# Setup of a two-block layer kernel: modulation pieces in the order 0, 2, 1, 3, two projection units by halves of the inner index, and part of the late pieces summed on TensorE

## The reference, cut to what matters

```python
for l in range(DEPTH):
    ada = jax.nn.silu(c) @ w_ada[l] + b_ada[l]          # (1, 1024) @ (1024, 6144)
    sh1, sc1, g1, sh2, sc2, g2 = jnp.split(ada, 6, axis=-1)
    h = x * (1.0 + sc1) + sh1
    y = mixer_ab(h, w_in_ab, ...)                       # starts with h @ w_in, (256, 1024) @ (1024, 3072)
```

## Time and profile before

| | |
|---|---|
| median of 3 runs | 1678.25 us (1677.92 to 1686.55) |
| the profiled execution, its own time | 1678.13 us |
| its span | 1676.3 us, so 1.8 us lie around it |
| PE busy | 1612.7 us, 96% of the span |
| DVE busy | 1085.5 us, 65% |
| ACT busy | 804.9 us, 48% |
| first projection matmul starts | 44.35 us into the span |

### The profile page before, as it was taken

The page is one execution under the profiler, slowest core; times in us unless marked ns, Lnnn a source line. Parts: engine busy times, 40 slices in busy tenths (PEclk is TensorE's granted clock), DMA queues, the critical chain, the costliest instruction groups (busy, mean ns, idle before and its releaser), DMA issues.

```text
span 1676.3 us, 24647 instructions
## 1 busy us (share of the span) xinstructions
PE 1612.7 (96%) x9268; PEld 1347.2 (80%) x9268; DVE 1085.5 (65%) x1329; ACT 804.9 (48%) x1033; POOL 224.8 (13%) x300
## 2 busy tenths in 40 slices
PE   3999999998999999999999999999999999999999
PEld 2997788878887788778888978888888889878887
DVE  7788878877758546664556896454554546765554
ACT  1565534336555343454446655434454445664433
POOL 2101001000000000068936200000000002200000
PEclk9999999999999999999999999999999999999999
DMA  9976787884644755465554425555465554345552
GB/s 320 335 250 202 274 297 280 283 290 130 212 148 143 276 191 185 151 189 183 192 176 138 166 81 179 194 182 193 157 201 192 184 192 164 138 160 178 197 179 98
DMA packets 225750, 330.10 MB, mean 197 GB/s; under 512 B 10423, under 2 KB 187160, under 8 KB 225678
## 3 DMA queue, kind: packets, MB, share of 16 engines
q1 hardware_dynamic: 210480, 276.93, 49.6%
q0 software_dynamic: 14800, 52.06, 8.9%
q10 hardware_dynamic: 398, 0.11, 0.0%
HBM read 327.97 MB, written 1.09 MB: 196 GB/s over the span
## 4 chain that ended last, share of the span: by engine, by line
PE 74%; DVE 13%; DMA 7%; ACT 3%; issue 2%; SPq 0%; POOLq 0%; POOL 0%; DVEq 0%; ACTq 0%
PE bank L2786 35%; PE bank L2530 20%; PE bank L2518 7%; DMA s_late<-in_w_ada 5%; DVE s_late L1916 4%; DVE s_wL L1898 3%; PE bank L2488 3%; PE bank L2798 1%; DVE s_late L1928 1%; ACT s_wH L1458 1%; DMA s_mix<-in_w_ada 1%; PE bank L2500 1%; DMA s_raw<-in_w_ffn_in 1%; PE bank L2629 1%; PE bank L2585 1%
## 5 line engine op out<-in xcount | busy, mean ns | idle before, releaser
L1898 DVE TENSOR_TENSOR s_wL<-s_raw,s_wH 128x2048 fp32r<-128x2048 f32 x254 | 587.1, 2312 | 296.1 <-ACT s_wH L1458 295.6
L1458 ACT ACTIVATE s_wH<-s_raw 128x2048 fp32r<-128x2048 f32 x254 | 485.2, 1911 | 229.6 <-PE bank L2786 144.8
L2786 PE MATMUL bank<-s_wH,s_hH 128*128 128x512 f32 x1056 | 420.7, 398 | 11.2 <-DVE s_hL L2252 8.7
L2786 PE MATMUL bank<-s_wH,s_hL 128*128 128x512 f32 x1056 | 412.6, 391 | 0.0
L2786 PE MATMUL bank<-s_wL,s_hH 128*128 128x512 f32 x1056 | 412.0, 390 | 0.0
L2786 PEld LDWEIGHTS bank<-s_wH,s_hH 128*128 128x128 f32 x1056 | 198.7, 188 | 55.8 <-issue 8.3
L2786 PEld LDWEIGHTS bank<-s_wH,s_hL 128*128 128x128 f32 x1056 | 198.5, 188 | 42.6
L2786 PEld LDWEIGHTS bank<-s_wL,s_hH 128*128 128x128 f32 x1056 | 199.0, 188 | 39.9 <-issue 0.7
L2530 PE MATMUL bank<-s_wH,s_aH 128*128 128x512 f32 x496 | 194.2, 392 | 1.1 <-DVE s_hL L2020 0.9
L2530 PE MATMUL bank<-s_wH,s_aL 128*128 128x512 f32 x496 | 193.2, 390 | 0.0
L2530 PE MATMUL bank<-s_wL,s_aH 128*128 128x512 f32 x496 | 193.0, 389 | 0.0
(11 more groups left out here) (453 smaller groups left out, 2245.8 us busy)
## 6 DMA issues: line engine op xcount, KB each, us to landing
s_raw<-in_w_ffn_in SPq DMA_DIRECT2D x88, 512.0 KB, 4.8
s_raw<-in_ffn_w_gate SPq DMA_DIRECT2D x88, 512.0 KB, 3.7
s_raw<-in_ffn_w_up SPq DMA_DIRECT2D x88, 512.0 KB, 4.6
s_raw<-in_ffn_w_down SPq DMA_DIRECT2D x88, 512.0 KB, 4.2
s_late<-in_w_ada POOLq DMA_DIRECT2D x20, 2048.0 KB, 9.9
s_raw<-in_w_ffn_out SPq DMA_DIRECT2D x44, 512.0 KB, 5.1
s_raw<-in_w_in_ab SPq DMA_DIRECT2D x24, 512.0 KB, 9.2
s_raw<-in_w_in_cd SPq DMA_DIRECT2D x24, 512.0 KB, 4.6
```

What stands on the lines that cost most here:

```text
L1458: A(wH[:, slot, :], raw[:, slot, :], ACT.Copy).then_inc(hi_ready, 1)
L1898: TTn(wL[:, slot, :], raw[:, slot, :], wH[:, slot, :].bitcast(F32), ALU.subtract).then_inc(lo_ready, 1)
L2786: last = mm(bank[GU_BANK[tt]][:], h, w[:, k, :], start=(half == 0 and k == 0 and i == 0), stop=(half == 1 and k == 3 and i == 2), skip_gro ...
```

## The change

It does four things.

1. Pieces are taken in the order 0, 2, 1, 3 (`FIRST_COLS`). After two of them shift and scale of the lower 512 features are known, and `modulated(0)` makes `h` for these; `modulated(1)` does the upper ones at the end.
2. The first two projection units are loaded, split and multiplied by halves of the inner index (`half_unit`, `split_half`). The first halves of both stand ahead of the late pieces on all engines, the second halves behind them.
3. Of the two late pieces DVE makes six of eight multiply-adds (`ON_VECTOR`); PE makes the other two from the raw weights (`first_rows`: 8 matmuls of one column, in the same form as the sum at L2564), into the same accumulator.
4. The order of loads changes to match: `x` in two halves of columns, 1 MiB of projection weights ahead of the late pieces, one half piece through the third slot of `raw`. The third unit is loaded when DVE has read that half piece. POOL's load of the bias table also waits for the last piece. 8 matmuls on zeros (`keep_busy`) stand ahead of the second halves.

```diff
+        FIRST_COLS, ON_VECTOR = (0, 2, 1, 3), (8, 8, 6, 6)
@@ SP
             first_ada(0)
             first_ada(1)
-            sp.dma_start(x[:], a["x"][0].rearrange("(a p) d -> p a d", p=P)).then_inc(ev("x_in"), 16)
+            sp.dma_start(x[:, :, 0:512], x_in[:, :, 0:512]).then_inc(ev("x_in0"), 16)
+            half_unit(0, 0, ab_units[0])
+            half_unit(1, 0, ab_units[1])
             first_ada(2)
+            sp.dma_start(x[:, :, 512:D], x_in[:, :, 512:D]).then_inc(ev("x_in1"), 16)
             first_ada(3)
-            qkv("ab", a["w_in_ab"][0])
+            sp.wait_ge(ev("first_hi"), 2)
+            half_unit(0, 1, ab_units[0])
+            half_unit(1, 1, ab_units[1])
+            sp.wait_ge(ada_step[1], 12)
+            straight("ab", ab_units, 2)
@@ POOL, ahead of the bias table
+            pool.wait_ge(ev("ada_in31"), 16)
@@ ACT
             first_ada(0)
+            split_half(0, 0)
             first_ada(1)
+            modulated(0)
+            split_half(1, 0)
...
             first_ada(2)
-            split_py(0)
+            split_half(0, 1)
             first_ada(3)
-            transposed("ab", ...)
-            split_py(1)
+            modulated(1)
+            split_half(1, 1)
             split_py(2)
@@ DVE
+            def modulated(half):
+                r, g = TR["ab"], 2 * half
+                dve.wait_ge(ada_out[0], half + 2)
+                dve.wait_ge(ada_out[1], half + 2)
+                sc = adaC[:, 0, 8 + 4 * half:12 + 4 * half]
+                step(TS(sc, sc, 1.0, None, ALU.add))
+                dve.sem_inc(ev("scale_ready"), 1)
+                dve.wait_ge(tr_done, TRD["ab"] + g + 1)
+                for c in (2 * g, 2 * g + 1):
+                    last = TS(t32[:, c, :], bank[TURN_BANK["ab"][g]][:, (c % 2) * T:(c % 2) * T + T], adaC[:, 0, 8 + c:9 + c],
+                              adaC[:, 0, c:c + 1], ALU.mult, ALU.add)
+                last.then_inc(t32_ready, 1)
+                if half == 0:
+                    split_half(0, 0)
+                lower_part(r, g)
+                lower_part(r, g + 1)
+                split_half(1, half)
...
-            ada(0, 1, 2)
+            modulated(0)
...
+            ada(0, 1, 2)
...
             ada(1, 1, 3)
...
-            split_py(0)
-            transposed("ab", ..., whole=False)
-            split_py(1)
+            split_half(0, 1)
+            modulated(1)
             split_py(2)
@@ PE
+            def first_rows(b):
+                pe.wait_ge(ev(f"ada_in{b}1"), 16)
+                pe.wait_ge(ada_out[b % 2], b // 2 + 1)
+                for u in range(4):
+                    for k in range(ON_VECTOR[b], KC):
+                        mm(bank[(0, 3)[b % 2]][:, u:u + 1], first_raw[b][1][:, k - KC // 2, u * P:u * P + P], silc[:, k:k + 1],
+                           start=(u == 0 and k == ON_VECTOR[b]), stop=False, skip_group_check=True)
...
+                if l == 0:
+                    half_unit(0, 0)
+                    half_unit(1, 0)
+                    first_rows(2)
+                    turn_columns(1)
+                    ada(0, 0, 1, False, begun=True)
+                    first_rows(3)
+                    ada(0, 1, 1, False, begun=True)
+                    pe.wait_ge(ev("lam_part"), 3)
+                    mm(bank[1][:, 384:385], ones[0:1, :], lam[0:1, 5:6], start=True, stop=True).then_inc(ev("lam_part"), 1)
+                    pe.wait_ge(ada_out[0], 3)
+                    keep_busy(0, 8)
+                    half_unit(0, 1)
+                    half_unit(1, 1)
+                else:
+                    dense(0, 16)
```

More of the change, by code:

```diff
@@ L1194, in qkv, with straight @@
                                  col_unit(w, m * 1536 + j * 256 + 512 * u))
-            def straight(name, units):
-                for u, src in enumerate(units):
+            def straight(name, units, first=0):
+                for u, src in enumerate(units[first:], first):
                     n = START[name] + u
@@ L1513, in pair_direct, with transposed @@
                 return A(blocks(hH[:, c, :]), backwards(bank[b][:, 0:T]), ACT.Copy)
-            def transposed(name, scale=None, offset=0.0, groups=4, direct=False):
-                for g in range(groups):
+            def transposed(name, scale=None, offset=0.0, groups=4, direct=False, first=0):
+                for g in range(first, groups):
                     if not direct:
@@ L2563, in ada @@
                     for u in range(4):
-                        last = mm(b[:, u:u + 1], acc[:, u * P:u * P + P], ones_col, start=True, stop=True)
+                        last = mm(b[:, u:u + 1], acc[:, u * P:u * P + P], ones_col, start=not begun, stop=True, skip_group_check=begun)
                     last.then_inc(ada_mm[slot], 1)
@@ L2587, in turn_tile, with turn_columns @@
                         last.then_inc(tr_done, 1)
+            def turn_columns(half):
+                pe.wait_ge(ev(f"x_in{half}"), 16)
+                for tt in range(TT):
+                    for k in range(KC // 2 * half, KC // 2 * half + KC // 2):
+                        at = (k % 2) * T + tt * P
+                        last = pe.transpose(bank[TURN_BANK["ab"][k // 2]][:, at:at + P], x[:, tt, k * P:k * P + P], ident[:])
+                        if tt and k % 2:
+                            last.then_inc(tr_done, 1)
             def transposed(name):
                 busy = BUSY[name] if name in BUSY else (0, 0)
-                if name in ("ab", "cd"):
+                if name == "cd":
                     keep_busy(TURN_BANK[name][0], busy[0])
@@ L2724, in ada_turn, with half_unit @@
                     ada(l, slot, cnt, slot == 0, b)
-                dense(0, 16)
+                def half_unit(u, half):
+                    pe.wait_ge(*((lo_ready, u + (LO0 + 1)) if half else (ev("first_lo"), u + 1)))
+                    H, L = (w[:, u, :].rearrange("p (k c) -> p k c", k=KC) for w in (wH, wL))
+                    for pair in (2 * half, 2 * half + 1):
+                        if u == 0:
+                            pe.wait_ge(tl_ready, 4 * TR["ab"] + pair + 1)
+                        for ft in range(2):
+                            for k in (2 * pair, 2 * pair + 1):
+                                wh, wl = H[:, k, ft * P:ft * P + P], L[:, k, ft * P:ft * P + P]
+                                for i, (w, h) in enumerate(((wh, hH), (wh, hL), (wl, hH))):
+                                    last = mm(bank[4 + u][:, ft * T:ft * T + T], w, h[:, k, :], start=(ft == 0 and k == 0 and i == 0),
+                                              stop=(k == KC - 1 and i == 2), skip_group_check=True)
+                    if half:
+                        last.then_inc(unit_used, 1)
+                if l == 0:
[14 more added lines that the diff above has]
+                    dense(0, 16)
                 if l == 1:
@@ L2730, in mixer @@
                     narrow(0).then_inc(ev("fd_mm"), 1)
-                dense(16, LEAD)
+                dense(16 if l else 32, LEAD)
                 for s in range(STEPS):
@@ L2938, in _ @@
             ada(0, 0, 0, False)
+            turn_columns(0)
             ada(0, 1, 0, False)
```

60 lines of the change are left out of this document (32 added, 28 removed).

## The result

The changed kernel takes 1683.96 us (median of 7 runs, 1680.92 to 1690.41); the kernel before took 1679.64 beside it (7 runs). The ratio over all runs, which is not the quotient of the two medians, is 1.0032, interval 1.0019 to 1.0044: 0.3% slower, small but clear of zero, where 0.3% faster was forecast. The profiled execution took 1681.74, its span 1679.9 us.

A forecast was written before the change was run, and what follows sets the result against it. PE, busy 96% of the span, bounds the kernel, so earlier projections pay: 5.9 us won at units 0 and 1, of which 5.0 kept (DVE 3.5 plus slack 1.5). 1678.13 - 5.0 = 1673.1 us, range 1671.5 to 1675 (0.45).

The forecast's parts named there:

- First halves from 28.0, done 35.9: Setup: first projection matmul at 28.0 us; the 48 first-half matmuls take 7.9 us at the old pace, to 35.9.
- DVE done with piece 3 at 40.6: DVE in the setup: finishes the last late piece at 40.6 us, 2.1 later than before.
- Pace between 36 and 48, 0.10 each: PE's thin work between the halves: one-column sums at the fast level, 0.10 us each; the step trusted least.
- the first rival's middle case: Clock falls in PE's thin work towards 39 to 42: start 45.5 to 48.5, gain 1 to 3.5, 1676; chance 0.25, shared.
- Second halves from 45.3, units done 52.1, gain 5.9: Projections: second halves start at 45.3 us; units 0 and 1 done at 52.1 instead of 58.04, bounds 4.8 and 6.9.
- First late load 2.7 to 4.0 earlier, landing after 12.0, DVE 3.5 earlier: Load issued behind unit 0: leaves 2.7 to 4.0 us earlier, takes 12.0; DVE, waiting for it, moves by 3.5.
- the sum's own bounds: Behind unit 0: its 24 second-half matmuls end at 48.2 to 49.5 us, the late load 2.7 to 4.0 earlier.
- The byte bound: Loads up to unit 6: by bytes carried, unit 6 lands 5.2 us earlier at 366 GB/s or 0.5 at 320.
- PE keeps 5.0 at the second turn: Second turn: DVE's 3.5 us plus a slack of 1.5 let PE move 5.0 us before it waits.
- I know of nothing behind it that is tied to the clock and not to PE, DVE or these loads: Rest of the kernel behind the second turn: later DVE waits have room, so the 5.0 us gain lasts.

The follow-up runs named there:

- e5: Changed kernel with 10 multiplications of zeros ahead of the second turn, one piece of the modulation left out of the output: 1680.36 us, 1.0010.
- e7: The changed kernel again, unchanged, for a second profile and ten more runs: 1684.07 us, 1.0029 against the kernel before.
- e10: Changed kernel with 40 one-column multiplications more, computing nothing, in PE's wait near 377 us, which they overran: 1690.14 us, 1.0064.
- e12: e10 with 10 multiplications of zeros ahead of the second turn: 1688.39 us, 1.0053.
- e14: Changed kernel with 16 one-column multiplications that compute nothing in PE's wait near 377 us: 1679.57 us, 0.9999 against the kernel before.
- e15: e14 with 10 multiplications of zeros ahead of the second turn: 1678.65 us, 0.9999 against the kernel before.
- e16: Changed kernel with 10 multiplications of zeros ahead of PE's wait near 446 us (second mixer, fourth turn): 1683.82 us, 1.0025.
- e18: e15 with 5 more multiplications of zeros ahead of the fourth turn of the second mixer: 1678.06 us, 0.9999 against the kernel before.
- e13: Kernel before with 16 one-column multiplications that compute nothing in PE's wait near 377 us: 1685.18 us, 1.0036.
- e2: Changed kernel without the 8 multiplications of zeros ahead of the second halves: 1682.22 us, 1.0019 against the kernel before.
- e9: Kernel before with 40 one-column multiplications more, computing nothing, in PE's wait near 377 us, which they overran: 1685.24 us, 1.0040.

## Why the prediction was wrong

By its own steps:

- **First halves from 28.0, done 35.9:** 28.82 and 36.8. Right; 0.8 late from the start, since half of `x` landed at 21.6.
- **DVE done with piece 3 at 40.6:** 41.7. Right within 1.1.
- **Pace between 36 and 48, 0.10 each:** wrong from 40.6 on, the step trusted least and the first rival's middle case: a fall at 39 to 42, a start at 45.5 to 48.5 and a gain of 1 to 3.5 at unit 2. The last sums reached DVE 1.94 us late, and the zeros held PE from 48.2, when the first of DVE's two lower parts was done, to 49.2 (by the chain; the timeline has the first matmul behind them begin at 48.66, overlapping the last of them).
- **Second halves from 45.3, units done 52.1, gain 5.9:** 49.2, 55.5, gain 2.5. The start is 3.9 late (1.1 for DVE's work, 1.9 for the late sums, 0.9 for the zeros); 0.5 came back because only the first 9 matmuls were slow.
- **First late load 2.7 to 4.0 earlier, landing after 12.0, DVE 3.5 earlier:** wrong in sign in both profiles of the changed kernel. By the sum's own bounds the least should have been 1.9, since 21 slow matmuls of the 24 end at 50.3, not 49.5. It left 0.4 later (53.92; unit 0 was done as late as before) and took 13.2; in other executions of this setup it left at 49.9 to 54.1 and took 10.3 to 12.4. The second late load left 2.6 us behind it instead of 5.5 and landed inside the same full stretch. The byte bound (0.5 us of gain) was nearer than the sum's 3.5.
- **PE keeps 5.0 at the second turn:** it kept 2.3 up to it and lost them to a wait that reached 2.4 us. The price of that wait was not in the sum: a fall of the clock behind it. In the nine profiles that have this setup (the changed kernel, e5, e7, e10, e12, e14, e15, e16, e18) unit 2 began 2.4 to 5.2 us earlier than before, and at 84 us, behind the second turn, they stood between 2.2 us ahead and 4.1 behind.
- **"I know of nothing behind it that is tied to the clock and not to PE, DVE or these loads":** this step decided the sign. TensorE's program grew by 16 f32 multiplications (two passes and two weight loads each) and 8 of zeros. The fetches behind it came earlier relative to the work: one into the late load of 431.45; near 1004, where a fetch came 0.7 us earlier, a second stall appears.

So two steps failed, each by some 5 us. The gain of 5.0 did not last: with the fetches moved (e14, e15, e18) the changed setup is level with the kernel before (0.9999 each, at widest 0.9988 to 1.0010), where the forecast was 0.997. And the code, a term that the sum did not have, cost the rest: 1.0029 to 1.0032 against 0.9999.

The sum with what was measured: the changed kernel is 0.7 to 1.4 us ahead at 422 (not all of it the setup's: 1.0 of the 1.4 came behind the wait near 377, where its clock fell for 3.4 us instead of 6.8); the slow load with its wait and clock takes 4.0 (38.1 to 42.1 us; 5.7 in e7); the second stall takes 1.8 (from 1.8 us behind at 985 to 3.6 at the end; 4.2 to 6.0 in e7). That is 1.4 - 4.0 - 1.8 = -4.4 for the profile shown, with 0.8 returned between; its span is 3.6 longer. e13 does the same to the kernel before and e14 undoes it. Shown: that moving the code moves the load, the wait and the time both ways. Shown in part: that the fetch holds up one engine's share of the load, by the row of single packets at its end. Argued only: why it does so, and that the fetches cause the stalls near 1004. Not told apart: how much of the 4.0 is wait and how much clock, and why e5 was better.

The page "Runtime: NRT & Kernel Launch" of the Trainium skill (section Instruction fetch mechanics) says that code streams in blocks of 16 KiB at a cost that is mostly hidden. The blocks agree (queue q8 of the changed kernel: 50 fetches, 0.82 MB, in the profile's page); the cost does not stay hidden here. "TensorE: Matmul & The Clock Gate" of the Trainium skill (HAM oscillation), weighed in the prediction, warned of the right outcome by another way. It speaks of a pause, and here the clock fell at 40.6 while PE was busy for 2.00 of 2.00 us with thin work. The prediction found no such pause in the trace of the kernel before; there is one, near 377 us, and the clock fell in it (PE's timeline, and its stretch of 380 to 388 us):

```profile
381.38 1.97 PE L2585 MATMUL bank<-s_ident,s_x 128*128 128x128 f32 x8 [4.48 <-DVE s_x L2191]
```

```profile
380.00:388.00 8.00, 6.62 (x30) 0.57 0.00 0
```

## What to carry to other kernels

A gain in one place must be followed to the next wait that another engine sets; here most of what PE won before 80 us became a wait, in the profiled execution with a fall of the clock as the price. When a change adds or removes instructions on an engine that never rests, look at its instruction fetches in the DMA view before explaining a difference of a few us far from the edit. Test it with harmless instructions of the same number in a wait: on the old kernel to make it slow, on the new one to repair it. And see first that they fit the wait: in f32 each counts twice.

## What the runs showed of the hardware

- One-column sums and transposes, back to back, PE busy 2.00 of 2.00 us: the granted clock fell to the lower level at 40.6 (41.2 in e7, 39.7 in e2), and with six 512-column multiplications among them at 42.5. In e9 it fell at 376.0 while 80 one-column passes ran (PE 2.00 of 2.00 us, 0.50 in 376 to 378).
- The profile's granted clock reads 1.00 until its first record; the pace (0.21 us a matmul until 33.65 in the changed kernel) shows that it was the lower level.
- A 16 KB instruction fetch 1.9 to 6.2 us into a 2 MB load went with a landing 0.6 to 2.2 us later (9.7 to 10.6 against 8.4 to 9.1 us, 8 profiles against 12), and one 7.7 us into a load of 8.4 us did not. The late part is a row of single packets, 0.22 us apart.
- Waits of PE of 2.3 to 3.2 us near 446 us were followed by a fall each time they were not filled (7 profiles); those of 1.0 to 1.7 in 4 profiles of 10.
